# Two of four prompt state products moved behind the output projection of a hybrid retention and mixture-of-experts layer

## The reference

```
h    = rms_norm(x) * (1 + scale1) + shift1
proj = h @ w_in                      # retention q|k|v|gate, attention q|k|v, two branch gates
ret  = retention(q, k, v, state)     # 4 heads, q and k 256 wide, v 512 wide
s_new[head] = s * g^L + sum_l (k[l] * decay[l])^T v[l]          # 256 x 512, an output
merged = sig(g1) * (ret @ w_br_ret) + sig(g2) * (attention @ w_br_diff)
x = x + gate1 * (merged @ w_out)
x = x + gate2 * moe(rms_norm(x) * (1 + scale2) + shift2)        # 16 experts, top 2 in one group
```

## Time and profile before

| | |
|---|---|
| runs | 1490.93, 1492.90, 1495.36 us, median 1492.9 |
| profiled execution | 1492.03 us, of which the span is 1489.8 |
| TensorE busy | 1461.5 us, 98% of the span |
| VectorE, ScalarE, GpSimd busy | 837.7, 659.5 and 303.2 us |
| granted TensorE clock, mean | 0.998 |
| moved by DMA | 304.61 MB |

### The profile page before, as it was taken

One profiled execution on the slowest core, in us unless ns is written; L12 is line 12 of the kernel. 1 busy time (PEld: TensorE's weight loads), 2 busy tenths in 40 slices (PEclk: granted clock), 3 DMA queues, 4 the chain that ended last, 5 costly groups with the idle time before them and its releaser, 6 DMA issues.

```text
span 1489.8 us, 21889 instructions
## 1 busy us (share of the span) xinstructions
PE 1461.5 (98%) x8004; PEld 1158.5 (78%) x8004; DVE 837.7 (56%) x1456; ACT 659.5 (44%) x1083; POOL 303.2 (20%) x181
## 2 busy tenths in 40 slices
PE   8999999999999999999999999999999999999998
PEld 6777787778777877787877677777888888887885
DVE  3532532253225222221866778655365899988998
ACT  5323312331233123322446545645233478888883
POOL 1352233224313431233000000000321100001004
PEclk9999999999999999999999999999999999999999
DMA  9646565555556455433441353245831799999996
GB/s 324 216 125 204 170 192 140 187 191 184 158 185 208 144 167 197 161 99 91 159 142 43 111 168 133 71 153 178 276 124 43 267 372 404 403 365 402 399 393 230
DMA packets 156460, 304.61 MB, mean 204 GB/s; under 512 B 16752, under 2 KB 54520, under 8 KB 155972
## 3 DMA queue, kind: packets, MB, share of 16 engines
q1 hardware_dynamic: 152548, 292.72, 58.2%
q0 software_dynamic: 3808, 10.49, 2.0%
HBM read 258.45 MB, written 47.86 MB: 206 GB/s over the span
## 4 chain that ended last, share of the span: by engine, by line
PE 45%; DMA 4%; DVE 2%; issue 1%; ACT 1%; POOL 0%; DVEq 0%; ACTq 0%; SPq 0%; POOLq 0%
PE pj L93 11%; PE pj L95 11%; PE pj L94 11%; DMA m_raw<-w 2%; PE d_B L2731 1%; PE d_B L2758 1%; PE d_B L2750 1%; DMA d_kc<-cache_diff_k 1%; PE d_B L2792 1%; PE d_B L2740 1%; PE d_B L2898 1%; PE d_B L2719 1%; PE d_B L1762 1%; PE d_B L2769 0%; PE pj L1745 0%
## 5 line engine op out<-in xcount | busy, mean ns | idle before, releaser
L93 PE MATMUL pj<-ring_hi,hT_hi 128*128 128x512 f32 x880 | 364.1, 414 | 3.7 <-ACT d_q_rows L2193 2.4
L95 PE MATMUL pj<-ring_hi,hT_lo 128*128 128x512 f32 x880 | 345.2, 392 | 0.0
L94 PE MATMUL pj<-ring_lo,hT_hi 128*128 128x512 f32 x880 | 344.0, 391 | 0.0
L546 POOL TENSOR_TENSOR ring_lo<-ring_raw,ring_hi 128x1024 fp32r<-128x1024 f32 x79 | 190.7, 2414 | 462.6 <-ACT ring_hi L628 462.5
L1622 DVE TENSOR_TENSOR m_lo<-m_raw,m_hi 128x1024 fp32r<-128x1024 f32 x188 | 222.1, 1221 | 18.8 <-ACT m_hi L1528 17.3
L628 ACT ACTIVATE ring_hi<-ring_raw 128x1024 fp32r<-128x1024 f32 x79 | 83.5, 1059 | 313.8 <-DMA ring_raw<-w_in 272.8
L1528 ACT ACTIVATE m_hi<-m_raw 128x1024 fp32r<-128x1024 f32 x188 | 192.0, 1058 | 19.9 <-DMA m_raw<-w 17.8
L93 PEld LDWEIGHTS pj<-ring_hi,hT_hi 128*128 128x128 f32 x880 | 166.2, 189 | 41.8 <-issue 8.9
L95 PEld LDWEIGHTS pj<-ring_hi,hT_lo 128*128 128x128 f32 x880 | 165.4, 188 | 36.1
L94 PEld LDWEIGHTS pj<-ring_lo,hT_hi 128*128 128x128 f32 x880 | 166.4, 189 | 29.3 <-issue 1.0
L853 DVE SCALAR_TENSOR_TENSOR r_S<-r_S,g,r_sm 128x512 f32<-128x512 f32 x64 | 45.0, 745 | 128.4 <-PE r_sm L1094 128.4
(11 more groups left out here) (403 smaller groups left out, 2507.4 us busy)
## 6 DMA issues: line engine op xcount, KB each, us to landing
m_raw<-w SPq DMA_DIRECT2D x188, 512.0 KB, 9.8
ring_raw<-w_in SPq DMA_DIRECT2D x72, 512.0 KB, 3.8
r_S<-state_ret SPq DMA_DIRECT2D x64, 256.0 KB, 4.7
r_ada_raw<-w_ada SPq DMA_DIRECT2D x16, 1024.0 KB, 6.6
o_state_s<-r_S SPq DMA_DIRECT2D x64, 256.0 KB, 3.3
a_raw<-w_ada SPq DMA_DIRECT2D x16, 512.0 KB, 8.7
ring_raw<-w_in SPq DMA_DIRECT2D x32, 256.0 KB, 3.4
ring_raw<-w_br_ret SPq DMA_DIRECT2D x16, 512.0 KB, 4.5
```

The costliest lines, as they stand in the source:

```text
L93: pe.matmul(out, s_hi, m_hi, start=start, stop=False)
L94: pe.matmul(out, s_hi, m_lo, start=False, stop=False)
L95: return pe.matmul(out, s_lo, m_hi, start=False, stop=stop)
L546: pool.tensor_tensor(lo[:, p], raw[:, p], hi[:, p].bitcast(F32), ALU.subtract).then_inc(lo_done, 1)
```

## The change

Heads 1 and 2 (`LATER`) no longer form their prompt state in phase R. SP stores the high and low parts of k and v to a scratch in DRAM that is not in use yet (`yg`, rows behind the first 512) after the next head's table load. ACT (before the copies of the next q and k) and DVE (before it writes `qkT` again) wait until these four stores have landed. In phase D they are loaded again, as soon as the last output columns release the memory, and the 2 x 24 products of the two states take the place of 43 of the fillers in the router stretch. ACT copies the results out and stores them from its own queue. Weight pieces 6 and 12, which lie over the parked data, wait until the states are done. In heads 1 and 2 the unit and the cross products of sample groups 2 and 3 move from step 1 to step 2 of the following QK projection.

```
+LATER = (1, 2)
+def later_home(io, i):
+    rows = io["yg"][4 * P + 6 * P * i:4 * P + 6 * P * (i + 1)]
+    return rows.rearrange("(p a) c -> p (a c)", p=P).rearrange("p (t c) -> p t c", t=NP_T)
...
+        if h not in LATER:
+            jobs += [("S", h, 0), ("S", h, 1)]
...
+        def stored_for_later(eng, h):
+            if h - 1 in LATER:
+                eng.wait_ge(later_out, 64 * (LATER.index(h - 1) + 1))
...
+            def store_later(h):
+                sp.wait_ge(kd_low, h + 1)
+                for t in range(NP_T):
+                    bank_taken(sp, f"V{h}", t)
+                home = later_home(io, LATER.index(h))
+                sp.dma_start(home[:, :, 0:RDK], kd_hi[:].bitcast(F32)).then_inc(later_out, 16)
+                sp.dma_start(home[:, :, RDK:2 * RDK], qk_r[:, 0:NP_T, 1].bitcast(F32)).then_inc(later_out, 16)
+                sp.dma_start(home[:, :, W:2 * W], v_hi[:, 0:NP_T].bitcast(F32)).then_inc(later_out, 16)
+                sp.dma_start(home[:, :, 2 * W:3 * W], v_lo[:].bitcast(F32)).then_inc(later_out, 16)
             def store_Sp(h):
+                if h in LATER:
+                    return
...
                             if g + 1 < RH:
                                 load_tab(g + 1)
+                            if g in LATER:
+                                store_later(g)
                         elif p == 2:
                             send_unit(u - 1)
...
+                    stored_for_later(act, h)
                     take(first, lambda t: qk[:, t].rearrange("p a c -> p (a c)"), ACT.Copy)
...
-                for d in range(2):
-                    take_state(h, d)
+                if h not in LATER:
+                    for d in range(2):
+                        take_state(h, d)
...
                 if h and t == ROPE_ORDER[0]:
-                    dve.wait_ge(Sp_out, 32 * h)
+                    dve.wait_ge(Sp_out, 32 * len([g for g in range(h) if g not in LATER]))
+                    stored_for_later(dve, h)
...
             def in_qk(h, u, i):
-                if i == 1:
+                if i == (2 if h in LATER else 1):
                     unit(u)
                     cross(h, 2)
                     cross(h, 3)
-                elif 2 <= i <= 5:
+                if 2 <= i <= 5:
                     steps(h, 4 + 2 * i)
...
-                state(h, 0)
-                state(h, 1)
+                if h not in LATER:
+                    state(h, 0)
+                    state(h, 1)
...
+    def load_later(self, sp, i):
+        for a in range(2):
+            s = slice(2 * a, 2 * a + 2)
+            sp.dma_start(self.later[i][:, s].bitcast(F32), later_home(self.io, i)[:, s]).then_inc(self.later_in[i][a], 16)
+    def late_state(self, pe, i, t):
+        if t % 2 == 0:
+            pe.wait_ge(self.later_in[i][t // 2], 16)
+        w = self.later[i]
+        for d in range(2):
+            s = slice(d * P, (d + 1) * P)
+            low = slice(RDK + d * P, RDK + (d + 1) * P)
+            last = mm3(pe, self.state_banks[i][d][:], w[:, t, s], w[:, t, low], w[:, t, W:2 * W], w[:, t, 2 * W:3 * W], t == 0, t == NP_T - 1)
+            if t == NP_T - 1:
+                last.then_inc(self.state_done, 1)
+    def take_states(self, act, i):
+        for d in range(2):
+            act.wait_ge(self.state_done, 2 * i + d + 1)
+            act.activation(self.states[i][d][:], self.state_banks[i][d][:], ACT.Copy).then_inc(self.state_taken, 1)
+        act.wait_ge(self.state_taken, 2 * i + 2)
+        for d in range(2):
+            act.dma_start(self.io["o_state_p"][0, 0, LATER[i], d * P:(d + 1) * P, :], self.states[i][d][:]).then_inc(self.state_out, 16)
...
+                if n in (6, 12):
+                    sp.wait_ge(self.state_done, n // 3)
...
+                if e == 0 and j == 0:
+                    act.wait_ge(self.state_out, 64)
...
             for e in range(EARLY):
                 slots(e)
+                if e == 0:
+                    pe.wait_ge(self.state_taken, 2)
                 stay_busy(2)
             turn_x(0)
             stay_busy(5)
+            pe.wait_ge(self.state_taken, 4)
...
             for t in range(NT):
+                if t == NT - 1:
+                    for i in range(len(LATER)):
+                        sp.wait_ge(w_done, 2 * NT - 1 + i)
+                        moe.load_later(sp, i)
                 sp.wait_ge(h2_done, 2 * t + 2)
...
             act.activation(s4[:, 1], s4[:, 0], ACT.Exp).then_inc(exp_done, 1)
+            moe.take_states(act, 0)
             act.wait_ge(shifted, 2)
             act.activation(s1[:, 5], s1[:, 4], ACT.Exp).then_inc(exp_done, 1)
+            moe.take_states(act, 1)
...
             turn_h2(3, 1)
-            pe.wait_ge(pj_free[3], LAST + 2)
-            stay_busy(8)
+            for b in (2, 3):
+                pe.wait_ge(pj_free[b], LAST + 2)
+            moe.late_state(pe, 0, 0)
             logits(3)
-            stay_busy(4)
+            moe.late_state(pe, 0, 1)
             for a in range(2):
                 turn_h2(4, a)
-            stay_busy(4)
             logits(4)
-            stay_busy(22)
+            for t in (2, 3):
+                moe.late_state(pe, 0, t)
+            for b in (0, 1):
+                pe.wait_ge(pj_free[b], LAST + 3)
+            for t in (0, 1):
+                moe.late_state(pe, 1, t)
             pe.wait_ge(assigned, 1)
...
             last.then_inc(pos_done, 1)
+            for t in (2, 3):
+                moe.late_state(pe, 1, t)
             pe.wait_ge(moe.tok_done, 1)
-            stay_busy(5)
             moe.run_pe(pe)
```

More of the change, by code:

```diff
@@ L188, in retention_order @@
         jobs += [("U", h, u) for u in range(8)]
-        jobs += [("S", h, 0), ("S", h, 1)]
+        if h not in LATER:
+            jobs += [("S", h, 0), ("S", h, 1)]
     pieces += ["GR1", "DQ0", "DK0"]
@@ L284, in phase_r @@
         u_in, m_out = sem("unit_in"), many("mod_parts_out", 2)
+        later_out = sem("later_out")
         by_set, parts_in, mod_sum, mods_out = map(sem, ("mod_by_set", "mod_parts_in", "mod_sums", "mods_out"))
@@ L536, in _ @@
             assert u == NU, u
-            sp.wait_ge(Sp_out, RH * 32)
+            sp.wait_ge(Sp_out, (RH - len(LATER)) * 32)
+            sp.wait_ge(later_out, 64 * len(LATER))
             for i in range(2):
@@ L1373, in __init__ @@
         self.U, self.V, self.Y, self.T, self.AT, self.X = banks[0], banks[1], banks[2:4], banks[4:6], banks[6], banks[7]
+        self.later = [nc.alloc_sbuf_tensor_at(f"m_later{i}", [P, NP_T, 3 * W], F32R, offset=(hT + 8192, wt)[i]) for i in range(len(LATER))]
+        self.states = [[nc.alloc_sbuf_tensor_at(f"m_state{i}_{d}", [P, W], F32, offset=base + 40960 + 2048 * (2 * i + d)) for d in range(2)]
+                       for i in range(len(LATER))]
+        self.state_banks = (banks[2:4], banks[0:2])
+        self.later_in = [many(f"later_in{i}_", 2) for i in range(len(LATER))]
+        self.state_done, self.state_taken, self.state_out = sem("state_done"), sem("state_taken"), sem("state_out")
         self.loaded0, self.hi0_done, self.lo0_done = many("first_loaded", 4), sem("first_hi_done"), sem("first_lo_done")
@@ L2886, in turn_h2 @@
                 last.then_inc(h_turned, 1)
-            def stay_busy(n):
-                for i in range(n):
-                    pe.matmul(pj[3][:, 0:P], K.ident[:], K.ident[:], start=True, stop=True)
             def logits(t):
```

## The result

The kernel became slower. After the change five runs took 1502.67 to 1508.08 us, median 1503.64; the kernel before, beside it on the same chip, took 1490.88 to 1495.36, median 1492.9. The ratio is 1.0077, with a 95% interval of 1.0063 to 1.0091. The profiled execution of after took 1503.64 us, its span is 1501.5 us (1489.8 before). Of the executions of the kernel before that stand beside the last four experiments, one took 1792.06 us at a granted clock of 0.764; the ratios leave it out.

A forecast was written before the change was run, and what follows sets the result against it. TensorE, busy 98% of the span, was taken as the bound. The terms -10.9 + 12.6 + 3.4 + 2.1 + 2.0 = +9.2 us on 1492.0 gave 1501.2, so 1502 against the runs' median; range 1491 to 1509.

The forecast's parts named there:

- rival 1: Stores push branch weights piece 2 and the wait for qk past TensorE's need: 1502, range 1498 to 1506; chance 0.56.
- Products: Phase R, heads 1 and 2: 24 state matmuls each leave TensorE, 2 x 5.44 = 10.9 us gained.
- Stalls: TensorE waits at the branch projections behind the delayed copies of q and k: 6.5 + 6.1 = 12.6 us.
- nothing moves that point: SP's table load before the stores was claimed to start 5.44 us earlier, like everything else.
- The chain behind it: ACT, from the start of piece 2's split to the first qk copy's end plus release: 2.1 us per head.
- The two ways of the delay: Before the qk copies: if weights passed the stores, the wait for the stores would still stall 3.7 and 3.3 us.
- rival 3: No change: stores at the spill's rate and clock holding, 1494, or weights overtaking the stores, +0.2 us; chance 0.18.
- The clock: Granted clock falls behind each branch projection stall: 1.7 us per head, 3.4 together, 0 if it holds.
- Cross products: QK projections, moved one step later, still wait for loads of S: 1.6 and 0.5 us, 2.1 together (0 to 3).
- Router: Router stretch: 43 fillers leave, 48 state matmuls come, making it 2.0 us longer (0.8 to 4).
- Expert phase: No term; the forecast counted itself wrong if something later there gave back or added more than 2 us.
- Two of the signs named in advance: Profile after: cross products of head 1 wait 1 to 2 us; slots(0) comes 1 to 2 us later after the logits.

The follow-up runs named there:

- the last four experiments: e5, e6, e7 and e8, run on another chip than the first four, beside nineteen runs of the kernel before (median 1491.93 us).
- e4: Changed kernel with the four stores issued some 21 us earlier, right behind the last load of S: 1487.21 us, ratio 0.9968.
- e2: Changed kernel with the four stores behind branch weights piece 2 in SP's order instead of ahead of it: 1501.06 us, ratio 1.0063.
- e3: Changed kernel with 26 filler matmuls of the identity on TensorE ahead of branch projections BR1 and BR2: 1497.64 us, ratio 1.0039.
- e1: Changed kernel with the unit and cross products of groups 2 and 3 back at step 1 in heads 1 and 2: 1513.96 us, ratio 1.0164.
- e5: e4 without parked loads, late products, copies and stores of states 1 and 2; the fillers of before are back: 1483.07 us, ratio 0.9935.
- e6: e4 with four fillers back in front of the last logits: 1486.81 us, ratio 0.9956.
- e7: e4 with state 0's third tile before the last logits and one tile of state 1, not two, behind the place sums: 1485.28 us, ratio 0.9952.
- e8: e6 with only head 2 moved, and head 1's cross products back at step 1: 1487.67 us, ratio 0.9977.

## Why the prediction was right

The forecast was 1502 in a range of 1491 to 1509, slower at 0.74; the median is 1503.64. The mechanism is the one of rival 1, and e4 shows it: with the stores elsewhere and nothing else changed, the loss is gone. By the prediction's terms:

- **Products.** Predicted -10.9; the steps in front of QK2 and QK3 are -5.26 and, without the clock's part, -5.44: -10.7.
- **Stalls.** Predicted 6.5 + 6.1 = 12.6. From the last start of QK plus its 0.23 us to the first of BR it is 6.85 and 7.00: 13.85. The step that was short is the landing of piece 2. Its delay was put at 8.2 us from the row with 383 GB/s. Piece 2 landed at 323.2, where the landing of before, moved by TensorE's -5.26 and +0.76, would be 314.4: 8.8 us; in head 2 by the same reckoning 9.0. The rate was not the larger part of this. Counted from SP's table load in front of the stores (312.46 and 457.19 before, 308.44 and 457.56 after), piece 2 lands 8.3 us later than before in head 1 and 8.5 in head 2, so 3.15 MB passed at 377 and 372 GB/s, near the 383 taken. The window 311.5 to 320 has 377 as well; the 349 of the window above includes the end of the stores of S and the table. The other 0.5 us is that the table load itself did not move with TensorE in full: the prediction's "nothing moves that point" was off by that much. Why it was is open. The Trainium skill (DMA: Bandwidth & Descriptors, Anatomy of one DMA) would give 7.2 us for the bytes, by a fit made for transfers that GpSimd issues, while these go out from SP; the measurement decides, 8.3 and 8.5. The two table loads that are in no row so far:

```profile
312.46 0.47 SPq L453 DMA_DIRECT2D r_tab<-tab_ret  x1
...
457.56 0.52 SPq L480 DMA_DIRECT2D r_tab<-tab_ret  x1
```

  The chain behind it was right: the split of piece 2 starts at 323.17, the first copy ends at 324.61 + 0.58, BR1 starts at 325.30; 2.13 us for the predicted 2.1.
- **The two ways of the delay.** Predicted was that without the queue order 3.7 and 3.3 us of stall remain. e2 has 5.29 and 5.10. This step was mis-sized: I took piece 2's bytes off the stores' 8.2 us, but in either order the same bytes have to pass. The copies of `qk` begin at 322.69 in e2, when the last store is there; piece 2 landed at 323.2 in after. So only the split and the last output tile are saved, 1.4 and 1.75 us by the stalls. The second half of rival 3, which used 7.0 us for this case, would not have come out at no change.
- **The clock.** Predicted 3.4 for both heads, measured 4.6 by e3 and 2.3 + 2.85 = 5.2 by the ledger's steps behind the stalls. The term was mis-sized: it was taken from a pause of 2.39 us, behind which some four us were slow. Behind the stall of 6.7 us the clock stayed at 0.50 from before the restart to about 330, so 11 and 13 matmuls took 0.43 us in place of 0.23. The eleven alone, from 325.30 to 330.13, took 4.83 us where 2.50 would do: the same 2.3 us without the ledger.
- **Cross products.** Predicted 1.6 + 0.5 = 2.1, measured 0.76 + 0.35 = 1.1. The price avoided was predicted as 3.4 us more a head; e1 has 4.46 - 0.76 = 3.7 and 4.64 - 0.35 = 4.3, and the clock behind them.
- **Router.** Predicted 2.0 (0.8 to 4), measured 2.57 to `slots(0)` and 0.91 behind it, 3.5. The predicted pieces were 0.4 us in front of the last logits and 1.2 us in front of `slots(0)`; they are 0.12 and 0.76 us. What I didn't have is 1.69 us between them: the clock fell behind the last logits in this trace. I had called the 24 state matmuls just covered by DVE's chain, at 0.227 us each. At 0.43 us for seven of them they are not. In e1 and e2, where the clock stayed, the same code costs 1.0 us to `slots(0)` and 1.1 and 0.9 behind it, about 2.0 as predicted. So the excess is one of the cases in which the clock fell. The fillers in front of logits(4) had been cover for a wait of 0.74 us, and I counted them only as time that could be filled otherwise; that they also held the clock is not shown.
- **Expert phase.** From the first turn of x to the end it is 315.7 before and 314.15 after, 1.6 us less. But it is 315.5 in e4, 314.3 in e5 (which has no parked data at all) and 315.3 in e6; e2 and e7 have 316.5 and 316.9. So this isn't a gift of the change: it is the scatter of that phase.

The terms sum to -10.7 + 13.85 + 5.2 + 1.1 + 3.5 - 1.6 = 11.35, and the ledger's end is 11.7; some 0.3 us are spread over phases R and D. The forecast of +9.2 came near because the products and the mechanism were right, and by some luck. All but one of the misses (cross products) were in the same direction, and the scatter of the expert phase took back 1.6 of them. Two of the signs named in advance came out otherwise: the wait at the cross products of head 1 was 0.76 us and not 1 to 2, and `slots(0)` came 2.57 us later after logits(2) and not 1 to 2.

What stays open: what decides between a kept and a lost clock behind the same pause, and whether fillers in front of the last logits change it. Also whether the 2 us between logits(2) and `slots(0)` that e7's trace has less than e4's show in the time of the whole: 1.6 of them are the clock, and the intervals overlap.

## What to carry to other kernels

A transfer put on a queue is paid by whatever stands behind it and by every engine that waits for its landing, so look for a place where its data is ready and the queue is slack: here that was 21 us earlier, and it turned +0.8% into -0.3%. When TensorE loses work, the loads that it waits for do not move with it, so move their first users back by as much. Idle matmuls aren't only time to be filled: before replacing them, ask which wait they cover. And before a difference between two traces is put down to an edit, look for the same instructions in the other traces: here 1.6 us of clock came and went without any edit there.

## What the runs showed of the hardware

- A pause of about the same length does not always take the clock. TensorE stood for 2.26 to 2.42 us in front of phase D in all ten traces. Behind it the granted clock fell in seven (0.56 and 0.58 before, 0.75 and 0.50 after, 0.58 and 0.56 in e4) and stayed at 1.00 in e1, e2 and e5. Up to there e4, e5, e6 and e7 are the same code, and only e5 kept it. That is worth 1.7 us between e4 and e5.
- A pause of only 0.74 us, with 16 matmuls of 20 columns behind it, was followed by a lower clock in after (0.60 and 0.55), e3 (0.59 and 0.55) and e4 (0.50 and 0.72), and by a full one in e1 and e2, with the same code in the router. It is worth 1.6 us (8.97 against 7.37). With four fillers in its place (e6, e8) and with six late matmuls there (e7) the clock stayed at 1.00, but e1 and e2 kept it without them.
- Four stores of 3.15 MB put the load behind them off by 8.3 and 8.5 us, 377 and 372 GB/s, close to the 383 of the nearest row. With the load in front of them (e2) the engine that overwrites their source waited 6.35 us instead.
